# One-hots of the PEER spread: gates multiplied in by VectorE, token by token, instead of by ScalarE

## The reference, cut to what matters

```python
s = jnp.einsum('thpd,hpkd->thpk', q, keys)            # two key halves, 128 scores each
sv, si = lax.top_k(s, 16)                             # 8 heads
cand = sv[:, :, 0, :, None] + sv[:, :, 1, None, :]
cv, ci = lax.top_k(cand.reshape(N, 8, 256), 16)
i1, i2 = ...                                          # the two halves of a pick's number, each below 128
eidx = i1 * 128 + i2                                  # 128 picks for each token
gate = jax.nn.softmax(cv, axis=-1)
h = gelu(einsum('tkd,td->tk', u_tab[eidx], x))
out = einsum('tk,tkd->td', gate * h, v_tab[eidx])
```

## Time and profile before

| | |
|---|---|
| profiled execution | 2137.83 us, its span 2135.9 us |
| mean granted TensorE clock of it | 0.949 |
| spread stage (steps 58 to 89) | about 1179 to 1400 us |
| TensorE matmuls, weight loads | 91%, 83% of the span |
| VectorE, ScalarE, GpSimd | 68%, 41%, 36% of the span |

### The profile page before, as it was taken

One profiled execution on the slowest core, in us unless ns is written; L12 is line 12 of the kernel. 1 busy time (PEld: TensorE's weight loads), 2 busy tenths in 40 slices (PEclk: granted clock), 3 DMA queues, 4 the chain that ended last, 5 costly groups with the idle time before them and its releaser, 6 DMA issues. The chain is left out here.

```text
span 2135.9 us, 29563 instructions
## 1 busy us (share of the span) xinstructions
PE 1938.0 (91%) x11347; PEld 1774.2 (83%) x11347; DVE 1453.0 (68%) x2546; ACT 884.5 (41%) x1762; POOL 768.6 (36%) x438
## 2 busy tenths in 40 slices
PE   4999689787898897889999999999969999999998
PEld 3999579687796696789999899999958888777776
DVE  3686554732403215999999999965548889888885
ACT  3356211223422114234434899954423344333433
POOL 0233132323530022157766455577712222222210
PEclk9899889788999999989999999999989999999999
DMA  4231101023642313159989799999999999999993
GB/s 130 65 79 53 47 1 31 1 94 103 203 159 85 113 30 94 41 189 359 361 334 342 278 372 373 374 408 399 408 374 397 400 400 397 398 399 400 400 398 115
DMA packets 211595, 512.99 MB, mean 240 GB/s; under 512 B 13312, under 2 KB 143104, under 8 KB 174592
## 3 DMA queue, kind: packets, MB, share of 16 engines
q1 hardware_dynamic: 172864, 259.43, 35.5%
q0 software_dynamic: 27648, 201.34, 23.6%
q10 hardware_dynamic: 10944, 50.34, 5.8%
HBM read 451.26 MB, written 59.80 MB: 239 GB/s over the span
## 5 line engine op out<-in xcount | busy, mean ns | idle before, releaser
L1863 POOL TENSOR_TENSOR ex_ulo<-ex_u,ex_uhi 128x1024 fp32r<-128x1024 f32 x128 | 307.0, 2402 | 246.4 <-ACT ex_uhi L1895 142.6
L1981 PE MATMUL ps<-xhi,ex_uhi 128*128 128x384 f32 x1024 | 353.9, 346 | 21.5 <-POOL ex_ulo L1863 16.3
L1981 PE MATMUL ps<-xhi,ex_ulo 128*128 128x384 f32 x1024 | 344.9, 337 | 0.0
L1981 PE MATMUL ps<-xlo,ex_uhi 128*128 128x384 f32 x1024 | 344.8, 337 | 0.0
L1514 POOL DMA_INDIRECT ga_ring<-in_uv,ga_idx x138 | 164.8, 1195 | 305.2 <-DVE found L1540 175.8
L2275 PE MATMUL ps<-po_vhi,po_whi 128*128 128x512 f32 x768 | 240.5, 394 | 28.2 <-DVE po_wlo L2309 26.8
L2275 PE MATMUL ps<-po_vlo,po_whi 128*128 128x512 f32 x768 | 238.0, 391 | 0.0
L2275 PE MATMUL ps<-po_vhi,po_wlo 128*128 128x512 f32 x768 | 237.8, 391 | 0.0
L1981 PEld LDWEIGHTS ps<-xhi,ex_uhi 128*128 128x128 f32 x1024 | 194.7, 190 | 23.7 <-POOL ex_ulo L1863 16.8
L2275 PEld LDWEIGHTS ps<-po_vhi,po_whi 128*128 128x128 f32 x768 | 143.4, 189 | 65.8 <-issue 35.7
L1981 PEld LDWEIGHTS ps<-xlo,ex_uhi 128*128 128x128 f32 x1024 | 194.8, 190 | 0.0
(11 more groups left out here) (408 smaller groups left out, 4270.9 us busy)
## 6 DMA issues: line engine op xcount, KB each, us to landing
ex_u<-in_uT SPq DMA_DIRECT2D x128, 512.0 KB, 7.7
scores<-in_peer_v SPq DMA_DIRECT2D x32, 1024.0 KB, 10.1
po_v<-in_peer_v SPq DMA_DIRECT2D x32, 1024.0 KB, 11.8
acts<-ex_h ACTq DMA_DIRECT2D x64, 384.0 KB, 7.9
gates<-scores ACTq DMA_DIRECT2D x12, 2048.0 KB, 12.3
scores<-acts SPq DMA_DIRECT2D x32, 768.0 KB, 12.6
scores<-gates SPq DMA_DIRECT2D x32, 768.0 KB, 15.8
in_w_raw<-in_w_in SPq DMA_DIRECT2D x24, 512.0 KB, 4.0
```

The costliest lines, as they stand in the source:

```text
L1863: pool.tensor_tensor(ulo[:, j % 3], u[:, j % 3], uhi[:, j % 3].bitcast(F32), ALU.subtract).then_inc(low, 1)
L1981: mm = pe.matmul(ps[:, j % 2, 0:ND], w[:, j % 3, k, :], x[:, k, :], start=(k == 0 and n == 0), stop=(k == KT - 1 and n == 2))
```

## The change

VectorE's second comparison of a quad is replaced by four operations, one for each token. Each compares the row of 0 to 127 with the token's second halves and multiplies the outcome by the token's gates; both are per-partition operands of one column. ScalarE's `scale` and the semaphore `scaled` are gone, and TensorE's quad waits for `hots` in its place. The first comparison (L2129), the three buffers, the order of the picks and GpSimd's wait stay as they are.

```diff
-            def scale(q):
-                act.wait_ge(hots, q + 1)
-                for t in range(4):
-                    ins = act.activation(hot[q % 3][:, 1, t], hot[q % 3][:, 1, t], ACT.Copy,
-                                         scale=pickT[:, 2, 4 * q + t:4 * q + t + 1])
-                ins.then_inc(scaled, 1)
...
-                if j == FIRST_SPREAD:
-                    scale(0)
-                    scale(1)
...
-                    if 0 <= q < QUADS - 2:
-                        scale(q + 2)
...
             def quad(q):
-                pe.wait_ge(scaled, q + 1)
+                pe.wait_ge(hots, q + 1)
...
-                dve.tensor_tensor(hot[q % 3][:, 1], over(iota, 1, 4), last(pickT[:, 1, 4 * q:4 * q + 4].unsqueeze(2), P),
-                                  ALU.is_equal).then_inc(hots, 1)
+                for t in range(4):
+                    n = 4 * q + t
+                    ins = dve.tensor_scalar(hot[q % 3][:, 1, t], iota, pickT[:, 1, n:n + 1], pickT[:, 2, n:n + 1],
+                                            ALU.is_equal, ALU.mult)
+                ins.then_inc(hots, 1)
```

More of the change, by code:

```diff
@@ L1833, in peer_experts @@
         turned, turned_out = sem("ex_turned"), sem("ex_turned_out")
-        hots, scaled, spread_mm, spread_out = (sem("ex_hots"), sem("ex_scaled"), sem("ex_spread_mm"),
+        hots, spread_mm, spread_out = (sem("ex_hots"), sem("ex_spread_mm"),
                                                sem("ex_spread_out"))
```

## The result

| | median us | ratio to before, 95% interval |
|---|---|---|
| before, 15 runs | 2134.89 (2121.99 to 2150.79) | |
| changed, 15 runs | 2151.07 (2141.43 to 2161.4) | 1.0073 [1.0045, 1.0102] |

The changed kernel is 15.6 us slower (0.0073 x 2134.89; 9.6 to 21.8 by the interval). Its time lies within the range on record, but it is not the forecast, which was no change: it is rival 1, the second per-partition operand paid after the first, which had a chance of 0.28. The base of the forecast was the median of three executions, 2140.82 us; that of fifteen is 5.9 lower. The changed kernel's profiled execution took 2148.41 us, span 2146.4.

The account below looks back on a forecast made before the run. TensorE was taken to bound the stage at 6.85 us a step. From the profiled 2137.83 us, 32 steps x 0 - 0.8 gave 2137.0; on the median run, with about 1 us for late steps, 2141; 8-in-10 range 2137 to 2162.

Parts of the forecast that it names:

- rival 1: Every new VectorE instruction: second per-partition operand fetched after the first, 0.06 us each, step 7.43, 2159 us; chance 0.28.
- TensorE bounds the stage at 6.85 us: Expert loop steps 58 to 89: TensorE's own work sets the 6.85 us step; ScalarE, 98% busy, merely keeps up.
- ScalarE's scalings are worth 0 in steady state, 0.8 us once: Removing 384 scalings (123 us) beside TensorE's full stream gains nothing, except 0.8 us at the head of the stage.
- A step of VectorE is 4.31 + 12 s: VectorE's step in us, s being one new instruction's pitch; TensorE stays the bound up to s = 0.212.
- the term for the descriptors' stretch: In VectorE's step: 0.05 us kept because a comparison beside GpSimd's descriptor generation seemed to take 0.66, not 0.61.
- s = 0.20: Pitch in us of one new VectorE instruction, taken from one-operand rows, guessing the second operand is fetched beside the first.
- The signs of being wrong: Durations of 0.34 us or more, quads' weight loads waiting for VectorE, a 7.4 us step, VectorE at 100%.
- Rival 2: New VectorE instructions miss the fast pass, one element a cycle: 0.26 to 0.32 us each, 2159 to 2182 us; chance 0.06.
- Rival 3: VectorE instructions wait out GpSimd's descriptor generation, up to 0.96 us a step: step 7.67, 2166 us; chance 0.08.
- the 1.42 us row: Earlier trace: a 128x20 tensor_scalar on VectorE took 1.42 us, held until GpSimd's 2.4 us subtraction ended.
- Nothing gives the loss back: Behind the stage: TensorE's stretch, then v table loads, so any change in stage length stays in the end time.
- ScalarE keeps about 2.9 us of work in a step: ScalarE in the stage: 6.76 us of work a step, less three quads' scalings at 1.28 us each.

Follow-up runs that it names:

- no_scaling: The kernel before with ScalarE's scaling taken away and nothing in its place (gates left out): step 6.85 us, stage 218.0 us, ratio 1.002.
- two_quads_in_three: The kernel before with the four new instructions for two quads of three, ScalarE scaling the others: step 6.88 us, stage 219.9 us, ratio 1.0039.
- price_list: The changed kernel plus 60 tensor_scalar at the end of VectorE's work, with two, one or no per-partition operands at several widths; run once, stage 232.8 us.

## Why the prediction was right or wrong

- *TensorE bounds the stage at 6.85 us; ScalarE's 98% is a neighbour.* Right: no_scaling leaves the step at 6.85.
- *ScalarE's scalings are worth 0 in steady state, 0.8 us once.* Right. From TensorE's first expert load of the stage to its first quad it was 2.64 us before (1179.45 to 1182.09) and is 1.8 now (1173.22 to 1175.0).
- *A step of VectorE is 4.31 + 12 s, and decides from s = 0.212 on.* Right as a law: 7.30 measured with s = 0.257, where it gives 7.39. Of the 0.09 too much, 0.04 are comparisons that were 0.01 to 0.02 shorter, and 0.05 are the term for the descriptors' stretch, which was a misreading of the earlier trace rows: the comparison at 1261.03 lasted 0.68 like the others, and the next one started late, at 1261.69, when TensorE had let go of its buffer: a short wait for TensorE (shown with two_quads_in_three above). At 0.195 TensorE leads, at 0.257 VectorE does.
- *s = 0.20.* This step failed: "on the guess that the second operand is fetched beside the first". The second adds 0.059 us to the first's 0.061; nothing of it is hidden. (That a fetch takes this time is the prediction's picture; the runs show the price.) The nearest row had one operand; the case on which all hung was one that no row showed, and its room was 0.012 us. The slope and the fixed part taken from the earlier trace rows were right (0.20 foretold, 0.195 measured for one operand).
- *Rival 1: 0.26 and a step of 7.43, +17.8 us.* This is what happened, with 7.30 and +15.6. The range holds the result because it was laid out to hold this rival, not because the forecast was near: the changed kernel's median is 10 us above the forecast of 2141, on a base that came out 5.9 us lower. The signs of being wrong came as named: rows of 0.336 us (0.34), VectorE at 100%, a step of 7.30 (7.4).
- *Rival 2, the slow pass.* Out by price_list's 0.54 ns a column. Its price of 0.26 at the low end was equal to rival 1's, so that the result alone could not have told them apart.
- *Rival 3, VectorE and descriptors lock each other out.* Out: the four instructions from 1261.79 on lie under descriptor generation (1261.46, 1.23 us) and take 1.02 us, the undisturbed 1.03; the generation itself takes 1.23 us, as beside the comparisons before (1.22). The longest of the 256 in the group took 0.427 us. The rule of the Trainium skill (SBUF — State Buffer, Who interferes with whom), by which one side is shut out for a whole instruction, doesn't show here for descriptors. For GpSimd's subtraction the 1.42 us row stays the only one that bears it out: no tensor_scalar of the change meets a subtraction, and the first comparison of each step, a tensor_tensor that meets the last 0.2 us of one, is only 0.09 us longer (0.69 against 0.60).
- *Nothing gives the loss back.* Right: behind the stage the changed kernel lost 1.2 us more, price_list 4.4.
- *ScalarE keeps about 2.9 us of work in a step.* It was 3.4 (25.08 of 50 us in no_scaling), which decided nothing.

The Trainium skill (Vector Engine (DVE) Microarchitecture Reference, 5.2 Measured stream behaviour on trn2) gives about 75 ns for each instruction beside its columns. For instructions with immediates only, the run agrees: a row of 219 ns less the overlap of 0.08 is 0.14 us, 67 ns of columns and 72 more. With one per-partition operand the fixed part is 0.13, with two 0.19, which the section doesn't say.

## What to carry to other kernels

Moving work from a busy engine to one with room pays only up to that room, and only if the first engine was on the path; write both steps out and compare the room (here about 0.7 us a step) with the bounds of what is added before asking what is taken off. Price an instruction by its own operands: count its per-partition operands, and where two are needed for the first time, take the chance seriously that each is paid. If a stage tips over by a few per cent, spread over more steps the form can be carried without loss; here it was not shown to gain anything over the kernel before either.

## What was not expected of the hardware

- Each per-partition operand of a tensor_scalar costs VectorE about 0.06 us (0.061 the first, 0.059 the second, at 128 to 512 columns), as much as 115 columns at 0.52 to 0.54 ns each. A scaling by an immediate behind the comparison is free.
- Four small instructions beside descriptor generation of 1.23 us were not held up (1.02 us, 1.03 elsewhere), nor was a comparison of 128x512 (0.60 us).
- Stops of TensorE of 2.35 and 3.22 us were followed by a granted clock of 0.72 and 0.58 for 3 to 6 us in one execution; in another of the same code, stops of 2.35 and 3.55 us were not (1.00).
